# Centring the values before a chunked recurrence, with right sides and outputs split into pieces, in a two-layer RWKV-7 / RetNet trunk

## The chip, the core and the metric

One core of one Trainium2 chip runs the whole program. The time is that of the device, in microseconds (us), the median over runs. The same input is used before and after the change.

## The reference, cut to what matters

Layer 0 mixes tokens by RWKV-7 (16 heads of width 64, 256 tokens, model width 1024), then a dense SwiGLU; layer 1 is a retention mixer and eight experts of which each token uses two. The change is in the RWKV-7 mixer alone:

```python
def step(S, inp):                       # S: 64 x 64 for each head, t = 0 .. 255
    r_t, d_t, k_t, v_t, aa_t, bb_t = inp
    sa = einsum('bhvk,bhk->bhv', S, aa_t)
    S = S * d_t + sa[..., :, None] * bb_t[..., None, :] + v_t[..., :, None] * k_t[..., None, :]
    y = einsum('bhvk,bhk->bhv', S, r_t)
    return S, y
...
mean = jnp.mean(y, axis=-1, keepdims=True)          # group norm over each head's 64 values
var = jnp.mean(jnp.square(y - mean), axis=-1, keepdims=True)
y = (y - mean) * rsqrt(var + 64e-5)
y = y * gn_w + gn_b
bonus = jnp.sum(r * k * r_k, axis=-1, keepdims=True) * v
return ((y + bonus) * g) @ wo
```

The row index v of S is carried through unchanged: S and y are linear in the values v_t, so y minus its mean over the head is what the recurrence gives for values with their mean taken out.

## The kernel before, in words

Everything is float32; matmuls run on TensorE, and the stages follow one another: projections of the RWKV mixer, its recurrence (called the core here), its output projection, the SwiGLU, the retention layer, the experts. The change touches the core, about 95 to 207 us of the span.

**How the core is tiled.** The 256 tokens are four chunks (c = 0 to 3) of 64. Within a chunk the recurrence is a triangular system. Each piece of work on TensorE is a job; the string `order` (before.py, lines 415 to 418) lists the jobs by hand, as name:slot. A slot is a pair of PSUM banks (slot s is banks 2s and 2s + 1). TensorE runs the list in order; a job waits until its inputs are stored and until the job that had its slot before is stored out of PSUM (`slot_free`). VectorE and ScalarE each walk the same list in the same order and do the stores that are theirs (`stores`): VectorE those of M, N, W, Z, Q, S and the last H, ScalarE those of V, B, Y, G and the other H; X and U are split between the two. The names are:

- V0 to V7: value projection, a quarter of 128 tokens each (V0 to V3 the first 128 tokens), stored in `vtok_r`.
- M, N, then W and H: the inverse of the triangular system of chunks 0 and 1 (set 0) and of chunks 2 and 3 (set 1) in six levels; W0.3 is set 0, level 3. The last level is H0.6 and H1.6.
- Q: masked products of keys and queries of a chunk, in two halves. Z: the head sums of the bonus, in 2 tiles. B: four groups of transposed keys.
- X: right side of a chunk, an own part (Q times the chunk's values) and, for c > 0, a part from the state S of the chunk before. U: the solution, written over half of the values' tile `UV`. S: the state after the chunk. Y0, Y1: outputs of chunks 0 and 1, and 2 and 3; each has a part from the states (`state_part`) and a part from Q and `UV`. G0, G1: eight transposes each of the gated, normed output; G0 and G1 feed the output projection `mixer_output`.

**GpSimd** (lines 601 to 661) adds the unit diagonal to the seeds of both inverses (line 619, after N0 and after N1 are stored), scales the keys (line 623), copies the values into `UV` (line 633, four times, a chunk each), and works out the terms of bonus and gate (lines 640 to 644). After Y0 it takes part in the first group norm (lines 648 to 656).

**VectorE** has, beside its stores, two rounds of bonus products (`bonus`, line 1162, after W0.1 and W0.2); after S0 and S1 the decay of the stored state into a spare tile (`St[3]`, line 1265), which the next S store adds to; the first group norm in steps at given jobs (`gn_after`); and the second, from Y1 on, in eight steps (`group_norm`, lines 1169 to 1196). Before G1, TensorE runs `mixer_output(0)` and six eighths of `mixer_output(2)`, 14 products of 128x128 by 128x512.

**SyncE** loads the output weights in two series of eight transfers, each waiting for the one before it (line 550): the first begins when V7 is made, the second not before U1 is made.

## Time and profile before

| | |
|---|---|
| Median of 3 runs | 1593.13 us (1592.57 to 1596.49) |
| The profiled execution: its own time | 1586.79 us |
| Its span | 1584.7 us |
| TensorE busy | 1561.4 us (99%) |
| VectorE busy | 1238.3 us (78%) |
| ScalarE busy | 973.7 us (61%) |
| GpSimd busy | 67.0 us (4%) |
| Granted TensorE clock | 0.998 of full |

PE is TensorE, DVE is VectorE, ACT is ScalarE, POOL is GpSimd, SP is SyncE. In a row of a timeline the first number is the start in us from the span's start, the second the length in us, then engine, line, operation, tiles written and read, shapes, and how many instructions were merged; the bracket gives the idle time just before it and what ended it. Line 1638 is the helper through which all matmuls go, so its rows are told apart by shape and time. A float32 matmul stands as two instructions in the trace. "Issue" is idle time for which the trace shows no other engine as the reason. The profiled execution had a time 6.34 us below the median of the three runs.

### The profile page before, as it was taken

The numbers are of one execution on the slowest core, as the hardware profiler recorded it, in microseconds if no ns is written. First come the engines' busy times: TensorE is split into PE (matmuls) and PEld (weight loads), VectorE is DVE, ScalarE is ACT, GpSimd is POOL, SyncE is SP. The second block draws the span as 40 slices with busy tenths as digits, with TensorE's granted clock in tenths as the row PEclk, the third lists the DMA queues.
The fourth block names the chain that finished last, engine by engine and source line by source line (L and its number), as shares of the span: only waits on it lengthen the run. The fifth ranks groups of instructions, "written<-read, shape, count | busy, mean of one in ns | idle before, by whom it ended". The sixth has DMA issues, their size and how long they took to land.

```text
span 1584.7 us, 24868 instructions
## 1 busy us (share of the span) xinstructions
PE 1561.4 (99%) x9653; PEld 1297.1 (82%) x9653; DVE 1238.3 (78%) x984; ACT 973.7 (61%) x814; POOL 67.0 (4%) x34
## 2 busy tenths in 40 slices
PE   9999899999999999999999999999999999999997
PEld 7778758888998888888888888888888888888885
DVE  7594667774764457989988988988988988988995
ACT  1522345553424446787777777777777777777774
POOL 0043300000000000020000000000000000000200
PEclk9999999999999999999999999999999999999999
DMA  9121259856445525999999999999999999999991
GB/s 317 59 89 30 83 239 366 327 191 231 160 162 197 199 109 184 408 408 385 403 385 362 396 383 364 391 401 353 391 399 351 389 398 354 390 385 360 404 416 63
DMA packets 78588, 470.75 MB, mean 297 GB/s; under 512 B 7860, under 2 KB 8244, under 8 KB 26932
## 3 DMA queue, kind: packets, MB, share of 16 engines
q1 hardware_dynamic: 67860, 442.13, 72.5%
q10 hardware_dynamic: 9504, 23.37, 3.9%
q0 software_dynamic: 1152, 4.19, 0.7%
q8 instruction: 56, 0.92, 0.2%
q14 instruction: 16, 0.13, 0.0%
HBM read 450.27 MB, written 19.40 MB: 296 GB/s over the span
## 4 chain that ended last, share of the span: by engine, by line
PE 93%; DVE 5%; ACT 1%; issue 1%; DMA 0%; POOL 0%; DVEq 0%; SPq 0%; ACTq 0%; POOLq 0%
PE ps L1638 90%; PE ps L2206 2%; DVE mem L1162 1%; PE ps L2198 0%; DMA h<-x 0%; PE ps L1657 0%; DVE mem L1137 0%; ACT mem L760 0%; DVE mem L1145 0%; DVE mem L1134 0%; POOL mem L619 0%; DVE mem L1230 0%; DVE workr L1046 0%; PE ps L1857 0%; ACT work L876 0%
## 5 line engine op out<-in xcount | busy, mean ns | idle before, releaser
L1638 PE MATMUL ps<-pairs_r,workr 128*128 128x512 f32 x2856 | 661.6, 390 | 0.6 <-DVE workr L1380 0.6
L1638 PEld LDWEIGHTS ps<-pairs_r,workr 128*128 128x128 f32 x2856 | 534.8, 188 | 112.2 <-issue 1.1
L1638 PE MATMUL ps<-workr 128*128 128x512 f32 x2024 | 483.4, 393 | 0.0
L1638 PEld LDWEIGHTS ps<-workr 128*128 128x128 f32 x2024 | 375.5, 188 | 77.2 <-DVE workr L1607 0.4
L1544 DVE TENSOR_TENSOR workr<-ring,workr 128x2048 fp32r<-128x2048 f32 x167 | 380.9, 2291 | 52.7 <-ACT workr L958 52.5
L1544 DVE TENSOR_TENSOR pairs_r<-ring,pairs_r 128x2048 fp32r<-128x2048 f32 x165 | 374.0, 2290 | 18.1 <-ACT pairs_r L958 16.2
L958 ACT ACTIVATE pairs_r<-ring 128x2048 fp32r<-128x2048 f32 x165 | 316.9, 1922 | 109.4 <-PE ps L1638 103.9
L958 ACT ACTIVATE workr<-ring 128x2048 fp32r<-128x2048 f32 x167 | 319.3, 1917 | 43.5 <-PE ps L1638 36.2
L1083 DVE TENSOR_TENSOR pairs_r<-ring,pairs_r 128x2048 fp32r<-128x2048 f32 x68 | 155.9, 2292 | 110.3 <-ACT pairs_r L722 108.9
L1638 PE MATMUL ps<-mem 64*64 64x64 f32 (+7 forms) x3064 | 197.7, 260 | 8.0 <-issue 2.6
L722 ACT ACTIVATE pairs_r<-ring 128x2048 fp32r<-128x2048 f32 x65 | 124.5, 1916 | 124.5 <-PE ps L1638 121.5
L1638 PEld LDWEIGHTS ps<-mem 64*64 64x64 f32 (+3 forms) x3064 | 155.2, 147 | 48.7 <-issue 27.2
L1638 PE MATMUL ps<-workr,pairs_r 128*128 128x256 f32 (+1 forms) x1088 | 170.8, 318 | 0.9 <-DVE workr L1046 0.8
L1638 PEld LDWEIGHTS ps<-workr,pairs_r 128*128 128x128 f32 x1088 | 153.4, 189 | 17.9 <-DVE workr L1046 1.4
L963 ACT ACTIVATE workr<-ps 128x512 fp32r<-128x512 f32 x56 | 33.6, 600 | 72.3 <-PE ps L2206 67.3
L1574 DVE TENSOR_TENSOR work<-work,ps 128x512 f32<-128x512 f32 x56 | 38.3, 684 | 25.4 <-PE ps L1638 25.4
L830 ACT ACTIVATE work<-ps 128x512 f32<-128x512 f32 x22 | 13.2, 601 | 53.5 <-PE ps L1638 53.5
L1549 DVE TENSOR_TENSOR workr<-ps,workr 128x512 fp32r<-128x512 f32 x56 | 38.4, 686 | 6.2 <-ACT workr L963 6.2
L736 ACT ACTIVATE mem<-ps 128x512 f32<-128x512 f32 x12 | 6.9, 600 | 43.9 <-PE ps L1638 43.9
L2206 PEld LDWEIGHTS ps<-cst,work 128*128 128x128 f32 x224 | 27.8, 140 | 7.2
L2206 PE MATMUL ps<-cst,work 128*128 128x128 f32 x224 | 33.5, 272 | 0.0
L678 POOL TENSOR_TENSOR route<-route,cst 128x4 f32<-128x4 f32 x1 | 0.2, 198 | 781.6 <-DMA back<-work 781.6
(238 smaller groups left out, 654.8 us busy)
## 6 DMA issues: line engine op xcount, KB each, us to landing
ring<-mstream SPq DMA_DIRECT2D x336, 1024.0 KB, 7.1
ring<-pstream SPq DMA_DIRECT2D x65, 1024.0 KB, 5.0
mem<-rstream SPq DMA_DIRECT2D x27, 512.0 KB, 8.3
sent<-work ACTq DMA_DIRECT2D x6, 1024.0 KB, 8.0
back<-work ACTq DMA_DIRECT2D x6, 1024.0 KB, 11.5
mem<-rstream SPq DMA_DIRECT2D x16, 256.0 KB, 3.4
work<-sent ACTq DMA_DIRECT2D x7, 512.0 KB, 7.8
back<-work ACTq DMA_DIRECT2D x7, 512.0 KB, 9.1
```

Of the source, the lines that this page charges most:

```text
L722: act_f(pair(i)[0], unit(i), ACT.Copy).then_inc(s_hi, 1)
L736: act_f(dst[:, q * 512:(q + 1) * 512], take(j), function).then_inc(s_pe, 1)
L830: act_f(low2[:, f % 2], hidden_banks(f)[:, :, T:2 * T], ACT.Copy).then_inc(s_fc, 1)
L958: act_f(pair(i)[0], unit(i), ACT.Copy).then_inc(s_hi, 1)
L963: act_f(actTh[:, i % 2], ps[:, 6 + i % 2, :].rearrange("p (g s) -> p g s", g=4), ACT.Copy).then_inc(s_ga, 1)
L1083: V.tensor_tensor(pair(i)[1], unit(i), pair(i)[0].bitcast(F32), ALU.subtract).then_inc(s_lo, 1)
L1162: ins = V.scalar_tensor_tensor(out=fm(rT)[:, k, :], in0=fm(rT)[:, k, :], scalar=vec(V_RK, k), in1=fm(kmT)[:, k, :], op0=ALU.mult, op1=ALU. ...
L1544: V.tensor_tensor(pair(i)[1], unit(i), pair(i)[0].bitcast(F32), ALU.subtract).then_inc(s_lo, 1)
L1549: V.tensor_tensor(actTl[:, i % 2], ps[:, 6 + i % 2, :].rearrange("p (g s) -> p g s", g=4), actTh[:, i % 2].bitcast(F32), ALU.subtract).the ...
L1574: V.tensor_tensor(act[:, j % 2, :], s1[:, j % 2, :], ps[:, 2 * (j % 2) + 1, :], ALU.mult).then_inc(s_ma, 1)
L1638: ins = nc.tensor.matmul(*args, **kw)
L2206: ins = nc.tensor.transpose(ps[:, 6 + i % 2, g * P:(g + 1) * P], act[:, i % 2, g * P:(g + 1) * P], ident)
```

## The change

The mean over each head of the values is taken on VectorE (`value_mean`, after the stores of W0.4 and W0.5), and GpSimd subtracts it where it copied values before. The group norms have no mean and no centring any more. ScalarE squares both outputs right behind their stores. VectorE gates the second output beside that. The decay of the state goes to GpSimd (`decayed_state`). The own part of X1 to X3 and the state part of the outputs are items of the order of their own (I1 to I3, P0 and P1), which signal nothing. Order and slots of the jobs are new. Names of semaphores and the tile `vmean` are left out below.

```diff
@@ -410,18 +412,21 @@
-        order = """V0:2 V1:0 M0:1 N0:3 M1:2 V2:0 N1:1 W0.1:3 H0.1:2 V3:0 W0.2:1 Q0.1:3 H0.2:2 V4:0 W0.3:1 H0.3:2
-                   V5:3 W1.1:0 W0.4:1 H1.1:2 Z0:3 V6:0 H0.4:1 W1.2:2 V7:3 W0.5:0 H1.2:1 Z1:2 H0.5:3 Q0.0:0 Q1.0:1
-                   W1.3:2 H0.6:3 B3:0 X0:1 B1:2 H1.3:0 B2:3 B0:1 W1.4:2 U0:0 Q1.1:3 H1.4:1 S0:2 Q2.1:0 X1:3 W1.5:1
-                   U1:2 Q2.0:0 H1.5:3 Y0:1 S1:2 Q3.0:0 H1.6:3 X2:1 Q3.1:2 U2:0 S2:3 X3:2 U3:3 G0:1 Y1:0 G1:1"""
+        order = """V0:2 V1:0 M0:1 N0:3 V2:2 M1:0 W0.1:1 H0.1:3 V3:2 N1:0 W0.2:1 H0.2:3 V4:2 Q0.0:0 W0.3:1 H0.3:3
+                   V5:2 W1.1:0 H1.1:1 W0.4:3 V6:2 H0.4:0 W1.2:1 Q0.1:3 W0.5:2 Z0:0 H0.5:1 H1.2:3 V7:2 W1.3:0 B2:1
+                   H1.3:3 Z1:2 X0:0 H0.6:1 B1:3 W1.4:2 B3:0 Q1.1:1 H1.4:3 U0:2 B0:0 Q1.0:1 W1.5:3 S0:2 Q2.0:0
+                   I1:1 X1:1 P0:3 U1:2 H1.5:0 Q2.1:1 Y0:3 Q3.1:2 I2:0 S1:1 Q3.0:3 H1.6:2 X2:0 I3:1 U2:3 S2:2
+                   X3:1 P1:0 U3:3 G0:1 Y1:0 G1:1"""
         slot_of = {}
...
             slot_of[name[0], int(c), int(n or 0)] = int(s)
-        jobs = list(slot_of)
+        sequence = list(slot_of)
+        jobs = [j for j in sequence if j[0] not in "IP"]
         number = {j: n for n, j in enumerate(jobs)}
-        before = {j: next((i for i in reversed(jobs[:n]) if slot_of[i] == slot_of[j]), None) for n, j in enumerate(jobs)}
+        before = {j: next((i for i in reversed(sequence[:n]) if slot_of[i] == slot_of[j]), None)
+                  for n, j in enumerate(sequence)}
@@ -455,11 +460,8 @@
-        GN_STEPS = 8
-        gn_after = {number["Y", 0, 0]: (0,), number["U", 2, 0]: (1,), number["S", 2, 0]: (2,),
-                    number["X", 3, 0]: (3,)}
-        gn_square_after = number["Y", 0, 0]
-        gn_root_after = number["U", 2, 0]
+        gn_after = {number["Q", 3, 0]: (1,), number["U", 2, 0]: (2,), number["X", 3, 0]: (3,)}
+        gn_root_after = number["X", 2, 0]
@@ -629,9 +631,11 @@
                             pool.wait_ge(*done)
+                    pool.wait_ge(s_vm, c // 2 + 1)
                 r0 = 64 * (c % 2)
-                nc.gpsimd.tensor_copy(UV[r0:r0 + 64, c], vtok_r[r0:r0 + 64, c // 2, :].rearrange(
-                    "p (h v) -> p h v", h=NH)).then_inc(s_uv, 1)
+                nc.gpsimd.tensor_tensor(UV[r0:r0 + 64, c], vtok_r[r0:r0 + 64, c // 2, :].rearrange(
+                    "p (h v) -> p h v", h=NH), vmean[r0:r0 + 64, c // 2].unsqueeze(2).to_broadcast([64, NH, HN]),
+                    ALU.subtract).then_inc(s_uv, 1)
                 pool.wait_ge(s_uv, c + 1)
@@ -644,11 +648,17 @@
-            pool.wait_ge(s_gm0, 1)
-            nc.gpsimd.tensor_tensor(y0, y0, gsum.unsqueeze(2).to_broadcast([P, NH, HN]), ALU.subtract).then_inc(s_gc0, 1)
-            pool.wait_ge(s_gc0, 1)
+            def decayed_state(c):
+                for done in stored(("S", c, 0)):
+                    pool.wait_ge(*done)
+                nc.gpsimd.tensor_tensor(St[3], St[c], gC.rearrange("p (n c) -> p n c", c=NC)[:, :, c + 1:c + 2].to_broadcast(
+                    [P, NP, 64]), ALU.mult).then_inc(s_sg, 1)
+            decayed_state(0)
+            decayed_state(1)
             pool.wait_ge(s_cb, 2)
-            pool.wait_ge(s_gq0, 1)
+            pool.wait_ge(s_gq, 1)
             nc.gpsimd.tensor_tensor(y0f, y0f, gtok[:, 0, :], ALU.mult).then_inc(s_gg0, 1)
@@ -795,11 +805,12 @@
                                   jbank(j, half).rearrange("p (k s) -> p k s", k=4), ACT.Copy).then_inc(s_ygT, 1)
-                if number[j] == gn_square_after:
-                    a.wait_ge(s_gc0, 1)
-                    act_f(UV[:, 0].rearrange("p h v -> p (h v)"), yS[:, 0].rearrange("p h v -> p (h v)"),
-                          ACT.Square).then_inc(s_gq0, 1)
-                    a.preload_act_table(ACT.Sqrt)
+                if kind == "Y":
+                    a.wait_ge(s_ja, count[j, "a"])
+                    act_f(UV[:, 0].rearrange("p h v -> p (h v)"), yS[:, c].rearrange("p h v -> p (h v)"),
+                          ACT.Square).then_inc(s_gq, 1)
+                    if c == 0:
+                        a.preload_act_table(ACT.Sqrt)
                 if number[j] == gn_root_after or j == ("Y", 1, 0):
@@ -1166,56 +1177,50 @@
-            def group_norm(t, step):
-
-                y = yS[:, t]
-                yf = y.rearrange("p h v -> p (h v)")
-                tmp = UV[:, 0]
-                bc = lambda z: z.unsqueeze(2).to_broadcast([P, NH, HN])
-                if step == 0:
-                    for done in stored(("Y", t, 0)):
+            bc = lambda z: z.unsqueeze(2).to_broadcast([P, NH, HN])
+            def value_mean(t):
+                for m in range(4):
+                    for done in stored(("V", 4 * t + m, 0)):
                         v.wait_ge(*done)
-                    link(V.tensor_reduce(gsum, y, AX.X, ALU.add))
-                    link(V.tensor_scalar(gsum, gsum, 1.0 / HN, None, ALU.mult))
-                elif step == 1:
-                    link(V.tensor_tensor(y, y, bc(gsum), ALU.subtract))
-                elif step == 2:
-                    link(V.tensor_tensor(tmp, y, y, ALU.mult))
-                elif step == 3:
-                    link(V.tensor_reduce(gvar, tmp, AX.X, ALU.add))
-                    V.tensor_scalar(gvar, gvar, 1.0 / HN, GN_EPS, ALU.mult, ALU.add).then_inc(s_gv, 1)
...
+                link(V.tensor_reduce(vmean[:, t], vtok_r[:, t, :].rearrange("p (h v) -> p h v", h=NH), AX.X, ALU.add))
+                V.tensor_scalar(vmean[:, t], vmean[:, t], 1.0 / HN, None, ALU.mult).then_inc(s_vm, 1)
+            def group_variance(t):
+                v.wait_ge(s_gq, t + 1)
+                link(V.tensor_reduce(gvar, UV[:, 0], AX.X, ALU.add))
+                V.tensor_scalar(gvar, gvar, 1.0 / HN, GN_EPS, ALU.mult, ALU.add).then_inc(s_gv, 1)
+            def second_group_norm():
+                y, gated = yS[:, 1], UV[:, 1]
+                yf, gf = y.rearrange("p h v -> p (h v)"), gated.rearrange("p h v -> p (h v)")
+                for done in stored(("Y", 1, 0)):
+                    v.wait_ge(*done)
+                v.wait_ge(s_cb, 2)
+                V.tensor_tensor(gf, yf, gtok[:, 1, :], ALU.mult).then_inc(s_gg1, 1)
+                group_variance(1)
+                v.wait_ge(s_gs, 2)
+                rsqrt(gvar, gsd, gsum)
+                v.wait_ge(s_gg1, 1)
+                link(V.tensor_tensor(gated, gated, bc(gsd), ALU.mult))
+                V.tensor_tensor(yf, gf, vtok_r[:, 1, :], ALU.add).then_inc(s_yg[1], 1)
...
                 y = yS[:, 0]
-                if step == 0:
-                    for done in stored(("Y", 0, 0)):
-                        v.wait_ge(*done)
-                    link(V.tensor_reduce(gsum, y, AX.X, ALU.add))
-                    V.tensor_scalar(gsum, gsum, 1.0 / HN, None, ALU.mult).then_inc(s_gm0, 1)
-                elif step == 1:
-                    v.wait_ge(s_gq0, 1)
-                    link(V.tensor_reduce(gvar, UV[:, 0], AX.X, ALU.add))
-                    V.tensor_scalar(gvar, gvar, 1.0 / HN, GN_EPS, ALU.mult, ALU.add).then_inc(s_gv, 1)
+                if step == 1:
+                    group_variance(0)
                 elif step == 2:
                     v.wait_ge(s_gs, 1)
-                    v.wait_ge(s_gc0, 1)
                     rsqrt(gvar, gsd0, gsum, s_gr0)
...
                     yf = y.rearrange("p h v -> p (h v)")
-                    link(V.tensor_tensor(y[:, 8:16], y[:, 8:16], gsd0[:, 8:16].unsqueeze(2).to_broadcast([P, 8, HN]), ALU.mult))
+                    link(V.tensor_tensor(y[:, 8:16], y[:, 8:16], bc(gsd0)[:, 8:16], ALU.mult))
                     v.wait_ge(s_cb, 2)
@@ -1258,20 +1263,18 @@
                     else:
+                        v.wait_ge(s_sg, c)
                         V.tensor_tensor(new, St[3], b3, ALU.add).then_inc(s_jd, 1)
-                    if c < NC - 2:
-                        g = gC.rearrange("p (n c) -> p n c", c=NC)[:, :, c + 1:c + 2].to_broadcast([P, NP, 64])
-                        v.wait_ge(s_jd, count[j, "d"])
-                        link(V.tensor_tensor(St[3], new, g, ALU.mult))
                 elif j == ("G", 1, 0):
...
                                   jbank(j, 1).rearrange("p (k s) -> p k s", k=4)).then_inc(s_ygT, 1)
+                if j in (("W", 0, 4), ("W", 0, 5)):
+                    value_mean(n - 4)
                 if number[j] in gn_after:
...
                 elif j == ("Y", 1, 0):
-                    for step in range(GN_STEPS):
-                        group_norm(1, step)
+                    second_group_norm()
             quarter_add(1, 0)
@@ -1817,6 +1820,19 @@
+            def own_part(job):
+                slot_free(job)
+                c = job[1]
+                wait_stored(("Q", c, 0))
+                wait_stored(("Q", c, 1))
+                pe.wait_ge(s_uv, c + 1)
+                for hd in range(NH):
+                    to, p_ = rows_at(hd % 2, c % 2), hd // 2
+                    ins = M(jbank(job, hd % 2)[to, p_ * 64:(p_ + 1) * 64], Qm[c][:, place(hd), 0:64], UV[:, c, hd, :],
+                            start=(p_ == 0), stop=(c == 0), skip_group_check=True)
+                return ins
             def state_part(job):
@@ -1829,18 +1845,24 @@
-            for j in jobs:
+            for j in sequence:
                 kind, c, n = j
...
                     pe.wait_ge(s_ygT, 2)
-                    wait_stored(("X", 3, 0))
+                    wait_stored(("S", 2, 0))
                     mixer_output(0)
...
                     pe.wait_ge(s_pe, first_in[slot_of[j]])
-                if kind != "Y":
+                if kind == "P":
+                    state_part(j)
+                    continue
+                if kind == "I":
+                    own_part(j)
+                    continue
+                if kind != "Y" and not (kind == "X" and c):
                     slot_free(j)
@@ -1886,14 +1908,9 @@
                 elif kind == "X":
-                    wait_stored(("Q", c, 0))
-                    wait_stored(("Q", c, 1))
-                    pe.wait_ge(s_uv, c + 1)
-                    for hd in range(NH):
-                        to, p_ = rows_at(hd % 2, c % 2), hd // 2
-                        ins = M(jbank(j, hd % 2)[to, p_ * 64:(p_ + 1) * 64], Qm[c][:, place(hd), 0:64], UV[:, c, hd, :],
-                                start=(p_ == 0), stop=(c == 0), skip_group_check=True)
-                    if c:
+                    if c == 0:
+                        ins = own_part(j)
+                    else:
                         wait_stored(("S", c - 1, 0))
@@ -1901,8 +1918,6 @@
                     up = slice(64 * (1 - c % 2), 64 * (1 - c % 2) + 64)
-                    if c == NC - 1:
-                        state_part(("Y", 1, 0))
                     wait_stored(("H", c // 2, LEVELS))
@@ -1912,14 +1927,12 @@
                     if c == 0:
-                        wait_stored(("B", 3, 0))
+                        wait_stored([i for i in jobs if i[0] == "B"][-1])
                     for hd in range(NH):
...
                 elif kind == "Y":
-                    if c == 0:
-                        state_part(j)
                     wait_stored(("U", 2 * c + 1, 0))
```

## Rows read from the trace of the kernel before

**Rows 1.** The chain that ended last: shares of the span by engine.
```profile
PE 93%; DVE 5%; ACT 1%; issue 1%; DMA 0%; POOL 0%; DVEq 0%; SPq 0%; ACTq 0%; POOLq 0%
```

**Rows 2.** Stretches: ends, length, busy us of PE, PEld, DVE, ACT, POOL; PE's clock.
```profile
99.00:192.42 93.42, 85.47 (x2532) 76.62 (x2522) 57.50 (x58) 23.93 (x32) 41.60 (x15) 1.00 0.16 47
...
194.44:206.72 12.28, 12.28 (x34) 5.54 (x31) 9.69 (x13) 1.24 (x2) 0.00 (x0) 1.00 0.01 2
206.72:228.00 21.28, 21.12 (x77) 11.43 (x74) 10.13 (x14) 10.32 (x19) 0.00 (x0) 1.00 0.89 361
```

**Rows 3.** Waits of PE, 99 to 192.42 us: total us, times, longest.
```profile
PE ps L1638 <- issue: 2.6, 4, 1.0
PE ps L1638 <- DVE mem L1250: 1.7, 1, 1.7
PE ps L1638 <- DVE mem L1230: 1.2, 2, 0.6
PE ps L1638 <- DVE mem L1253: 0.9, 1, 0.9
PE ps L1638 <- DVE mem L1241: 0.8, 1, 0.8
```

**Rows 4.** Timeline, start of the core: PE reaches W0.1 (the second row is W0.1).
```profile
97.81 8.29 PE L1638 MATMUL ps<-mem 128*128 128x256 f32 x274
106.50 1.75 PE L1638 MATMUL ps<-mem 64*64 64x64 f32 x105 [0.39 <-POOL mem L619]
```

**Rows 5.** Timeline of POOL.
```profile
102.55 3.81 POOL L619 TENSOR_TENSOR mem<-mem 128x2048 f32<-128x2048 f32 x1 [18.03 <-DVE mem L1236]
...
111.25 5.51 POOL L623 TENSOR_TENSOR mem<-mem,small 128x3072 f32<-128x3072 f32 x1
...
159.47 4.55 POOL L644 TENSOR_TENSOR mem<-mem 128x2048 f32<-128x2048 f32 x1
180.46 2.36 POOL L652 TENSOR_TENSOR mem<-mem 128x1024 f32<-128x1024 f32 x1 [1.26 <-ACT mem L800]
188.00 1.04 POOL L655 TENSOR_TENSOR mem<-mem,small 128x512 f32<-128x512 f32 x1 [5.18 <-DVE small L1036]
```

**Rows 6.** Timeline of DVE: the first bonus products.
```profile
108.86 10.53 DVE L1162 SCALAR_TENSOR_TENSOR mem<-mem,par 128x256 f32<-128x256 f32 x4
```

**Rows 7.** Line 1137 (DVE, beside POOL's 3.64 us memset): min/median/max ns, starts.
```profile
L1137 DVE TENSOR_SCALAR mem<-mem,par x8: 326/344/3682, 80.7 to 85.9; 128x256 f32<-128x256 f32 x8
```

**Rows 8.** Timeline, stores of W1.2, V7, W0.5 and Z1.
```profile
138.80 1.23 DVE L1241 TENSOR_TENSOR mem<-ps,mem 128x1024 f32<-128x1024 f32 x1 [5.44 <-PE ps L1638]
142.43 0.39 ACT L779 ACTIVATE mem<-ps 128x256 f32<-128x256 f32 x1 [3.53 <-PE ps L1638]
143.55 1.23 DVE L1241 TENSOR_TENSOR mem<-ps,mem 128x1024 f32<-128x1024 f32 x1 [3.52 <-PE ps L1638]
...
146.33 0.17 DVE L1228 COPY small<-ps 128x16 f32<-128x16 f32 x1 [1.55 <-PE ps L1638]
```

**Rows 9.** Timeline of DVE and ACT, from after Y0's store to X2's.
```profile
175.79 1.22 DVE L1204 TENSOR_REDUCE small<-mem 128x16 f32<-128x1024 f32 x1 [4.87 <-ACT mem L792]
...
177.84 1.91 DVE L1265 TENSOR_TENSOR mem<-mem,small 128x512 f32<-128x512 f32 x1
179.23 1.06 ACT L800 ACTIVATE mem<-mem 128x1024 f32<-128x1024 f32 x1 [3.48 <-POOL mem L648]
...
182.17 0.69 DVE L1250 COPY mem<-ps 64x512 f32<-64x512 f32 x1
```

**Rows 10.** Timeline, first and last of the second group norm, and G1.
```profile
195.61 1.22 DVE L1178 TENSOR_REDUCE small<-mem 128x16 f32<-128x1024 f32 x1 [3.73 <-ACT mem L792]
...
204.74 1.23 DVE L1196 TENSOR_TENSOR mem<-mem 128x1024 f32<-128x1024 f32 x1
206.56 1.04 PE L1935 MATMUL ps<-cst,mem 128*128 128x128 f32 x8
```

**Rows 11.** Timeline of SP: the 16 transfers of the output weights.
```profile
142.42 48.76 SPq L550 DMA_DIRECT2D mem<-rstream  x16
```

18 lines of the change are left out of this document (5 added, 13 removed).

## The prediction

> **What bounds the kernel now.** I read the chain that ended last first: 93% of the span is TensorE, 5% VectorE [rows 1]. So a change in the core is worth what it does to TensorE's idle time there, and nothing else. I then cut the core into stretches [rows 2]. From 99.00 to 192.42 us, where Y1 begins, TensorE is busy 85.5 of 93.4 us: 8.0 us idle. From 194.44, after Y1, to 206.72 it is busy throughout, with the 14 products placed before G1, and then to 228.00 it idles 0.16 us. All that this change can win from waits lies in those 8.0 us, 0.5% of the time. The waits [rows 3] say whose they are: 2.6 us are "issue", with no engine behind them, and 4.6 us in the four rows of VectorE's stores (lines 1250, 1230, 1253, 1241); the remaining 0.8 us are one wait on GpSimd's seeds of 0.39 [rows 4], one at G0, and rounding. No clock is at stake: it is 1.00 in every stretch [rows 2].
>
> TensorE's work is the same after the change: I and P are parts that stood inside X, U and Y. So time after minus time before is idle after minus idle before, over the same list of jobs. I walk the new order and write down each wait.
>
> **Lengths that the walk uses.** V7 takes 142.43 - 138.80 = 3.6 us, W0.5 1.1 us, H1.2 with Z1 2.8 us [rows 8]; I take 1.1 for each W, H, Q, U, S and part of X, 1.85 for Z, 2.2 for Y and for P1. A full VectorE store is 1.22 to 1.23 us, V's on ScalarE 0.39 [rows 8], half a store of X or U 0.69 [rows 9]. About 0.05 us pass from a job's end to its store, 0.14 from a store to the waiting job (182.17 + 0.69, then the next job at 183.01).
>
> **The start, +1.05 us.** W0.1 begins at 106.50, released by GpSimd's seeds, whose addition starts at 102.55 and lasts 3.81 [rows 4, 5]. That start hangs on N0, which keeps its place. Before, TensorE has M1, V2 and N1 to do in the meantime and waits 0.39. The new order has moved N1 behind V3, so that it waits 0.39 + 1.05 = 1.44 us. The job is not saved, only later.
>
> **Bonus products against GpSimd, -0.4 us.** Four instructions of 0.47 us at the least took 10.53 us [rows 6], while GpSimd ran line 619, line 623 (5.51 us, from 111.25) and two copies back to back [rows 5]; the delay of a store made waits at 119.8 and 122.7 of 0.82 and 0.57 us. With N1 later, the first bonus round (after W0.1, 108.95) meets an idle GpSimd. The second is hit: N1 is made at 106.5 + 2.2 + 0.4 (issue) + 3.6 + 1.1 = 113.8, stored at 115.0, GpSimd then runs 3.81 + 5.51 to 124.4, and the bonus ends at about 125.7. Behind it on VectorE are the stores of Q0.0 (to 126.9) and W0.3 (to 128.1). TensorE meanwhile goes through W0.2, H0.2, V4, Q0.0, W0.3, H0.3, V5 to 126.2 and wants the slot of Q0.0 for W1.1: it waits 0.8, then 0.15 for W0.3's. Sum 0.95, instead of 1.39.
>
> **Value means, +2.2 us.** The first (two instructions, 1.22 [rows 9] and 0.17) follows W0.4's store while TensorE has V6 and H0.4, 4.7 us, before it needs VectorE: nothing. The second is placed after W0.5, but it needs V4 to V7, and V7 comes four jobs later. VectorE stands there; behind it in its queue is the store of Z0, whose slot 0 W1.3 needs, and W1.3 is TensorE's next job after V7. So TensorE stands for 0.05 + 0.39 (V7's store) + 0.05 + 1.22 + 0.02 + 0.17 + 0.17 (Z0's copy) + 0.14 = 2.2 us. Nothing covers it: all that could run in it is behind W1.3. GpSimd's subtraction in place of the copy costs between 1.04 (line 655, half the elements) and 2.36 us (line 652) each [rows 5]; I take 1.9; the first two end near 139, X0 comes near 154, the last two are needed by I2 thirty us later: nothing.
>
> **The tail, +0.1 us.** Before, VectorE carries a reduction and its scaling (1.4 us) and the decay (1.91) between Y0 and the stores that TensorE wants [rows 9], and TensorE waits 1.7, 0.9, 0.7 (issue) and 0.3 there, with 0.6 near 161.5 (line 1230). The new order frees VectorE of those 3.3 us. GpSimd's chain up to line 644 ends near 173 (it took 17.3 us from Z1), then the decay of S0, 1.04 by line 655's row [rows 5], and S1 needs it near 181: hidden. But the variance (1.22 + 0.17) stands after Q3.0 in front of H1.6's store. Count from the start of Q3.1: I2 to 2.1, S1 3.2 (stored 3.95), Q3.0 4.3 (stored 5.6), H1.6 5.4, X2 6.5, I3 7.55. GpSimd decays S1 to 5.15 and gates Y0 until 7.6 (2.36 [rows 5]). VectorE reduces 5.6 to 6.85; its small scaling meets GpSimd. One row shows such an instruction stopped 3.68 us by GpSimd's memset [rows 7], so I let it end at 7.75. Then H1.6's store to 9.0, X2's to 9.65, and U2 starts at 9.8: 2.25 us of wait. S2 follows U2 at once and waits for its store, 0.05 + 0.69 + 0.14 = 0.9, and X3, whose own part I3 is already spent, waits the same 0.9 for S2. Waits of VectorE in the tail: 4.05 us, against 1.7 + 0.9 + 0.6 + 0.3 = 3.5 and 0.4 of other small ones that the new order also covers, together 3.9.
>
> A reduction beside a GpSimd instruction stands in no row; the bounds are 0 (as the stores with one input in PSUM, 1.22 us beside POOL) and 1.25 us more on H1.6's store, were it held until 7.6 like the row of line 1137. I take 0. The Trainium skill, "SBUF — State Buffer", section "Who interferes with whom", says that on trn2 a reduction never contends with GpSimd while a scaling by a constant can; by it the sum stays as I have it, and if it is wrong here the time is that of the second rival below. No row before tests it.
>
> **After Y1, nothing.** The second group norm goes from 195.61 to 205.97 [rows 10]. Reduction, scaling, centring and square, 3.8 us, leave it, a square on ScalarE (1.06 [rows 9]) comes in beside the gating. But the 14 products last until 206.72, later than the norm already, and G1 follows them in TensorE's queue in both kernels. What is late next is TensorE itself: the 3.8 us are worth 0. Were the 14 products not there, they would all count. Output weights: the series takes 48.76 us and its last transfer about 3 [rows 11], from V7's end. V7 is 4.5 us later (146.9), so the end is near 198.5. U1 is also later (173), but the first series lasts until 175. The first use is at Y1's end + 7.0 us, 204: 5 us of cover; without it each us late would count fully.
>
> **Sum.** Issue idle 2.6 is kept: where it falls depends on where code runs out, and I bound it by 0 and 5.2. Changes: +1.05 - 0.45 + 2.2 + 0.15 = +2.95, and about 0.25 for small waits that a tighter list has: +3.2 us. The profiled run took 1586.79 us, so 1590.0 for one like it. The median of the runs shown is 6.34 higher; on it the change gives 1593.13 + 3.2 = **1596.3 us**, 0.2% more.
>
> **Rivals.**
> First, the late stores are swallowed: TensorE does not stand after V7 and before U2, because VectorE, emptied of the means' and decays' work, catches up before TensorE arrives. It would need TensorE to be 2 us slower through H0.5, H1.2 and V7 than 1.1 + 1.1 + 3.6. For it: VectorE is busy 57.5 of 93.4 us only [rows 2]. Against: the order of waits in the queue, which no spare time of VectorE alters. It decides where V7's wait is below 0.2 us. Price 2.2 + 2.25 saved: 3.2 - 4.45 = -1.3, 1591.8 us, faster than before. The floor is all of the waits on stores gone, -4.6 - 0.4: 1588.1.
> Second, reductions contend as well: U2 waits 1.25 more, 1597.6.
> Third, code arrives late more often: the front of the core is denser in small jobs than before, and pauses double: +2.6, 1598.9.
> Fourth, the change does not do what it says to TensorE's order, since other waits than these set the pace: 0, 1593.1.
>
> **Chances.** Forecast 0.50, first rival 0.20, second 0.10, third 0.10, fourth 0.10. A measurement of this kernel can tell about 0.3%, 4.8 us, from no change. Below 1588.3 only the floor gets: 0.04. Above 1597.9: the third rival and the upper edge of the second and of the forecast, 0.16. Within: 0.80. The range, 1590.5 to 1599.5, takes in the first rival's 1591.8 and the third's 1598.9; the forecast's own is 1594.5 to 1597.9.
>
> **What would show it.** TensorE's idle time before Y1's last part 11 us, not 8. A wait of 1.4 us on line 619's successor near 105; VectorE's idle until V7's store and a 2.2 us wait of TensorE behind the copy of Z0; one bonus instruction of over 5 us; two waits of 0.9 at S2 and X3 and one of 2 at U2. G1 straight behind the products, with the norm done 3 us before. If the idle time falls below 8 us the forecast is wrong, whatever else holds; if V7's wait is there and the sum still falls, the tail was misread.

## The result

The changed kernel takes 1593.65 us (median of 20 runs, 1591.24 to 1597.47), beside 1591.82 us of the kernel before in 20 runs on the same chip. The ratio is 1.0017, with an interval of 1.0009 to 1.0025: 2.7 us more by the ratio (the two medians differ by 1.8), slower than before by less than the 0.3% that were called no change. The forecast was +3.2 us, and 1596.3 us in all.

The profiled execution of the changed kernel took 1594.91 us (span 1593.1). That of before took 1586.79, so the two profiles are 8 us apart where the medians are 2 apart. The granted clock of the whole run tells why: 0.992 in this one, 0.998 in that one.

The shares of the chain that ended last, for the changed kernel:

```profile
PE 95%; DVE 2%; ACT 1%; issue 0%; DMA 0%; POOL 0%; DVEq 0%; SPq 0%; ACTq 0%; POOLq 0%
```

And its stretches, with the columns of [rows 2] (ends, length, busy us of PE, PEld, DVE, ACT, POOL, PE's clock, DMA share, GB/s). The first holds the core up to Y1 and a little of the products behind it, the second the products before G1, the third the output projection:

```profile
99.00:199.00 100.00, 90.95 (x2589) 81.65 (x2579) 54.92 (x58) 25.18 (x34) 44.58 (x16) 0.95 0.15 45
199.00:211.10 12.10, 12.10 (x31) 5.36 (x30) 5.75 (x9) 2.29 (x3) 0.00 (x0) 1.00 0.01 2
211.10:232.50 21.40, 21.29 (x77) 11.59 (x75) 10.08 (x14) 10.27 (x19) 0.00 (x0) 1.00 0.88 357
```

TensorE idles 9.05 us in the first, against 8.0 before [rows 2]. The second and third are as before but for 0.2 us. What is new is the eighth number: TensorE had 0.95 of its clock in the core, where it had 1.00. TensorE's waits in that stretch (total us, times, longest) are these:

```profile
PE ps L1641 <- issue: 2.2, 3, 1.1
PE ps L1641 <- DVE small L1233: 2.1, 1, 2.1
PE ps L1641 <- DVE mem L1255: 2.0, 1, 2.0
PE ps L1641 <- DVE mem L1258: 0.9, 1, 0.9
PE ps L1641 <- DVE mem L1267: 0.8, 1, 0.8
PE ps L1641 <- POOL mem L621: 0.6, 1, 0.6
PE ps L1641 <- DVE mem L1235: 0.3, 1, 0.3
```

Beside [rows 3], what is new are two waits of 2 us, one behind V7 and one in front of U2; before, the longest was 1.7. The timeline of the first (start, length, engine, line, operation, and in brackets the idle time before it with its releaser):

```profile
147.59 0.38 ACT L789 ACTIVATE mem<-ps 128x256 f32<-128x256 f32 x1 [2.62 <-PE ps L1641]
148.11 1.22 DVE L1187 TENSOR_REDUCE small<-mem 128x16 f32<-128x1024 f32 x1 [7.40 <-ACT mem L789]
149.36 0.17 DVE L1188 TENSOR_SCALAR small<-small 128x16 f32<-128x16 f32 x1
149.44 0.17 DVE L1233 COPY small<-ps 128x16 f32<-128x16 f32 x1
149.66 1.56 PE L1641 MATMUL ps<-mem 64*64 64x64 f32 x64 [2.11 <-DVE small L1233]
```

This is the walk of the prediction instruction for instruction. VectorE idles 7.40 us until V7 is stored, reduces, scales, copies Z0, and only then TensorE may go on. What follows it is the surprise. The same stretch cut into microseconds, with only length, TensorE's busy time, its clock, DMA share and GB/s as columns:

```profile
148.00:149.00 1.00, 0.00 (x0) 1.00 0.38 88
...
150.00:151.00 1.00, 1.00 (x58) 0.61 0.01 2
151.00:152.00 1.00, 1.00 (x13) 0.50 0.42 131
152.00:153.00 1.00, 1.00 (x16) 0.50 0.36 125
153.00:154.00 1.00, 1.00 (x60) 0.68 0.07 23
154.00:155.00 1.00, 1.00 (x24) 1.00 0.26 68
```

TensorE stands until 149.66, works, and between 150 and 151 is put to 0.50 of its clock, 1.2 instead of 2.4 GHz, until after 153. The granted clock falls after the wait, not in it. Summed as one minus the clock over the four lines, the fall comes to 1.7 us on top of the wait's 2.1. On the same work it cost 1.5: from the end of this wait to the transposes of B1 TensorE took 8.54 us (149.66 to 158.20), and 7.04 (148.94 to 155.98) in a kernel below in which no fall follows. The same comes again in the tail:

```profile
186.83 1.22 PE L1641 MATMUL ps<-mem 64*64 64x64 f32 x32 [2.02 <-DVE mem L1255]
188.93 1.98 PE L1641 MATMUL ps<-mem 128*64 128x64 f32 x32 [0.88 <-DVE mem L1258]
191.69 4.32 PE L1641 MATMUL ps<-mem 64*64 64x64 f32 x128 [0.78 <-DVE mem L1267]
```

U2, S2 and X3 wait 2.02, 0.88 and 0.78 us. S2's 32 instructions take 1.98 us; at full clock they took 1.15 in the run with both moves below. The clock is 0.50 from 188 to 194, which over TensorE's busy time sums to 2.6 us. The work itself, the three rows above, took 7.52 us instead of 5.73 in the run with both moves: 1.8 us more.

### The profile page after: what moved, and what is told of

It reads as the page before. It is cut to its first block, busy times and chain, and to the rows that moved or that the text cites. A ratio compares the mean times of both kernels' runs of the same rounds, so it can differ in the third digit from the quotient of the medians.

```text
span 1593.1 us, 24870 instructions
## 1 busy us (share of the span) xinstructions
PE 1570.0 (99%) x9653; PEld 1305.8 (82%) x9653; DVE 1231.9 (77%) x980; ACT 974.0 (61%) x815; POOL 68.6 (4%) x35
## 4 chain that ended last, share of the span: by engine, by line
PE 95%; DVE 2%; ACT 1%; issue 0%; DMA 0%; POOL 0%; DVEq 0%; SPq 0%; ACTq 0%; POOLq 0%
PE ps L1641 92%; PE ps L2219 2%; DVE mem L1173 1%; PE ps L2211 0%; DMA h<-x 0%; PE ps L1660 0%; PE ps L1879 0%; POOL mem L621 0%; PE ps L2148 0%; DVE workr L1057 0%; ACT work L887 0%; DVE work L1375 0%; DVE mem L1241 0%; DVE mem L1235 0%; DVE h L1615 0%
## 5 line engine op out<-in xcount | busy, mean ns | idle before, releaser
L1641 PE MATMUL ps<-mem 64*64 64x64 f32 (+6 forms) x3064 | 200.7, 265 | 9.5 <-issue 2.2
```

Source lines behind the costliest of these rows:

```text
L1641: ins = nc.tensor.matmul(*args, **kw)
```

## The experiments

**Theory A:** the change adds two long waits of TensorE, and each costs its own length and a stretch at half clock behind it; the places alone decide. **Rival B:** the granted clock falls now and then in any run, wherever it likes, and the profile after happened to catch two falls. Both explain the 8 us between the profiles; they differ in what a kernel without the long waits would do. A single profile's fall can be chance, so the clocks of all runs are set side by side at the end. The first four kernels take away one wait, the other, both, and put a shorter one back.

**The mean of the second half later.** It stands behind W1.3, which runs after V7's store in any case; no work is left out.

```diff
-                if j in (("W", 0, 4), ("W", 0, 5)):
-                    value_mean(n - 4)
+                if j in (("W", 0, 4), ("W", 1, 3)):
+                    value_mean(c)
```

> Of the changed kernel, one placement is moved: VectorE takes the mean of the second half of the values after its store of W1.3 instead of after W0.5, so it no longer stands for V7 with Z0's copy behind it. Theory A (a wait of about 2 us also halves the granted clock for some 3 us behind it; in the changed kernel's trace the clock is 0.50 to 0.68 from 150 to 154 us, right behind the 2.11 us wait): the wait of 2.1 us goes and the granted clock stays 1.00 in the four us after V7, worth 2.1 + 1.7 = 3.8 us against the changed kernel; the second dip, at 187 to 195 us, stays. Ratio to the kernel before about 1.0017 - 0.0024 = 0.9993. Rival B (the clock dips come of themselves, wherever they fall): only 2.1 us go, a dip shows somewhere in the core all the same, ratio about 1.0004.

Measured: 1591.36 us, ratio 0.9997 [0.9986, 1.0008], which is 3.2 us under the changed kernel's ratio. The interval holds A's 0.9993 and B's 1.0004; the profile speaks for A. The wait behind V7 is gone and the clock stays at 1.00 there; the wait before U2 is 2.0 us as before, and the fall behind it is there (stretches of this kernel, columns as above):

```profile
144.00:154.00 10.00, 10.00 (x227) 8.85 (x223) 2.71 (x5) 3.26 (x5) 2.04 (x2) 1.00 0.18 56
184.00:195.00 11.00, 9.34 (x196) 8.88 (x197) 4.48 (x10) 1.54 (x3) 2.31 (x2) 0.53 0.31 96
```

**The variance later.** The other wait alone.

```diff
-        gn_after = {number["Q", 3, 0]: (1,), number["U", 2, 0]: (2,), number["X", 3, 0]: (3,)}
-        gn_root_after = number["X", 2, 0]
+        gn_after = {number["X", 2, 0]: (1,), number["S", 2, 0]: (2,), number["X", 3, 0]: (3,)}
+        gn_root_after = number["U", 2, 0]
```

> Of the changed kernel, one placement is moved: the variance of the first output is taken on VectorE after the store of X2 instead of after Q3.0, its root on ScalarE after U2, its reciprocal root after S2. The stores of H1.6 and X2 are then not held up. Theory A: U2's wait falls from 2.02 to about 0.2 us, the clock stays 1.00 from 187 to 195 us, worth 1.8 + 2.4 (dip of 0.5 to 0.88 over eight us, less the part of it in which TensorE waited) = 4.2 us at most, part of which comes back if G0 now waits for the norm, by up to 1.5 us; the dip behind V7 stays. Ratio to the kernel before about 1.0000. Rival B: 1.8 us less of wait and a dip all the same, ratio about 1.0006.

Measured: 1592.91 us, 1.0006 [0.9992, 1.0019], which is B's number, with A's 1.0000 inside the interval. The profile is the mirror image: U2's wait is 0.2, the tail runs at 1.00, and the fall behind V7 stays. The gain is smaller, as 0.9 us of it come back as a wait of G0, which needs the norm that was moved back; and the profile has one more fall, at 157.5 to 160.7, with no long wait ahead of it.

```profile
150.00:154.00 4.00, 4.00 (x104) 3.47 (x94) 1.23 (x1) 0.90 (x2) 3.11 (x2) 0.57 0.22 70
182.00:194.00 12.00, 9.60 (x336) 8.78 (x332) 9.54 (x15) 2.39 (x6) 6.04 (x4) 1.00 0.28 90
```

**Both later.** Both edits above.

> Both placements moved (the second mean after W1.3, the variance after X2). Theory A: no dip of the clock in the core at all, as in the profile of the kernel before; against the changed kernel 2.1 + 1.8 us of wait and about 1.7 + 2.4 us of clock less, some 7 to 8 us; ratio to the kernel before about 1.0017 - 0.0048 = 0.9970, 2.7 to 4.5 us faster than it. Rival B: the waits alone, ratio about 0.9993.

Measured: 1589.12 us, 0.9978 [0.9965, 0.9991]: 6.2 us less than the changed kernel, and faster than before. A's 0.9970 is inside the interval and B's 0.9993 just outside. Neither place has a fall. But A had forecast none in the core, and there is one at 141 to 145, in which TensorE never stood still:

```profile
182.00:196.00 14.00, 11.09 (x281) 9.22 (x277) 8.24 (x14) 5.02 (x8) 2.97 (x3) 1.00 0.28 93
141.00:145.00 4.00, 4.00 (x131) 3.83 (x127) 0.10 (x1) 1.62 (x2) 0.00 (x0) 0.57 0.01 4
```

**VectorE held for V7, with nothing to do there.** The kernel with both moves, and VectorE waits for V7's store after W0.5 as in the changed one, but does no reduction.

```diff
+                if j == ("W", 0, 5):
+                    for done in stored(("V", 7, 0)):
+                        v.wait_ge(*done)
```

> As the kernel with both placements moved, but VectorE still waits for the store of V7 after W0.5, with nothing to do there but the copy of Z0 behind it: TensorE waits 0.05 + 0.39 + 0.05 + 0.17 + 0.14 = 0.8 us instead of 2.1 behind V7. It is the same place with a shorter wait. Theory A, that the length of the pause decides: 0.8 us slower than the kernel with both moved and no dip of the clock. Rival C, that any pause at this place brings the dip (with the same work before it): 0.8 + 1.7 = 2.5 us slower, and a clock of about 0.57 over the four us behind V7.

Measured: 1590.67 us, 0.9988 [0.9977, 1.0000]. The wait is back at 0.68 us, without the reduction's 1.4, and no fall follows it. So the order of waits makes the hold and the reduction makes it long; that only the long one touches the clock rests here on one profile. In time the step from the kernel with both moves is 1.6 us with overlapping intervals, so that it decides between neither A's 0.8 nor C's 2.5.

```profile
148.94 1.16 PE L1644 MATMUL ps<-mem 64*64 64x64 f32 x64 [0.68 <-DVE small L1233]
```

**The kernel before, with the hold built in.** If A is right, a wait of 2 us put into the kernel before must bring the fall as well.

```diff
+                if j == ("W", 1, 2):
+                    for done in stored(("V", 7, 0)):
+                        v.wait_ge(*done)
+                    link(V.tensor_reduce(small[:, 224:240], ...))
+                    V.tensor_scalar(small[:, 224:240], small[:, 224:240], 1.0 / HN, None, ALU.mult).then_inc(s_hold, 1)
...
+                if j == ("W", 0, 5):
+                    pe.wait_ge(s_hold, 1)
```

> The kernel before with a pause put in and nothing else: behind V7, VectorE waits for its store, reduces the second half of the values into spare columns and scales them, as the changed kernel does, and TensorE waits for that before W0.5. The wait is 0.05 + 0.39 + 0.05 + 1.22 + 0.02 + 0.17 + 0.14 = 2.0 us. Theory A (a wait of about 2 us brings a dip of the granted clock right behind it, worth 1.7 us, on top of its own length): 3.7 us slower than before, ratio 1.0023, and clock 0.5 to 0.7 in the three to four us after the wait. Rival B (dips fall where they like, waits do not bring them): 2.0 us slower, ratio 1.0013, mean granted clock of the runs as before (0.9944).

Measured: 1597.42 us, 1.0039 [1.0023, 1.0056], +6.2 us. B's 1.0013 is outside the interval, and A's 1.0023 is its lower end. The wait came out at 2.80 us, not 2.0, and the timeline shows who took the 0.8:

```profile
143.00 2.14 POOL L634 COPY mem<-mem 64x1024 f32<-64x1024 f32 x2 [23.93 <-ACT mem L780]
144.13 1.04 DVE L1274 TENSOR_SCALAR small<-small 128x16 f32<-128x16 f32 x1
145.22 4.97 PE L1644 MATMUL ps<-mem 64*64 64x64 f32 x140 [2.80 <-DVE small L1274]
```

The scaling, 0.17 us by itself, ends when GpSimd's copies do. The clock then falls twice, from 145 to 149 and from 151 to 156, and a third time, from 189 to 193, behind the tail's wait, which was 1.71 us before and is 1.95 here. Two more waits are new or longer, of 1.3 us (on ScalarE, at 168) and 1.1 us (before G0, 0.3 in the kernel before), so that the 6.2 us are not those of one wait and its fall. This kernel's stretch:

```profile
144.00:156.00 12.00, 10.78 (x292) 10.41 (x296) 4.43 (x6) 2.05 (x2) 6.01 (x4) 0.72 0.30 92
```

**A new tail.** The kernel with the later mean, and H1.6 moved ahead of I2 and Q3.1 behind X2, so that the variance stands after H1.6's store and none that TensorE wants is behind it.

```diff
-                   I1:1 X1:1 P0:3 U1:2 H1.5:0 Q2.1:1 Y0:3 Q3.1:2 I2:0 S1:1 Q3.0:3 H1.6:2 X2:0 I3:1 U2:3 S2:2
+                   I1:1 X1:1 P0:3 U1:2 H1.5:0 Q2.1:1 Y0:3 H1.6:2 I2:0 S1:1 Q3.0:3 X2:0 Q3.1:2 U2:3 S2:2 I3:1
...
-        gn_after = {number["Q", 3, 0]: (1,), number["U", 2, 0]: (2,), number["X", 3, 0]: (3,)}
-        gn_root_after = number["X", 2, 0]
+        gn_after = {number["H", 1, 6]: (1,), number["U", 2, 0]: (2,), number["X", 3, 0]: (3,)}
+        gn_root_after = number["H", 1, 6]
```

> The changed kernel with the second mean after W1.3, and the end of the order rewritten so that each store in the chain S1, X2, U2, S2, X3 has a job beside it: Y0, H1.6, I2, S1, Q3.0, X2, Q3.1, U2, S2, I3, X3. The variance follows the store of H1.6, which now comes before S1. Expected waits of TensorE: U2 about 0.2, S2 about 1.05 (the store of Q3.1 stands in front of U2's), X3 and G0 none, so about 1.7 us less wait than in the kernel with both placements moved. Theory: ratio to the kernel before about 0.9978 - 0.0011 = 0.9967. Rival: if dips of the clock set the medians and not waits below 1 us, no difference to the kernel with both moved, 0.9978.

Measured: 1586.49 us, 0.9967 [0.9953, 0.9982], 5.3 us faster than before. That is the ratio forecast, but the kernel with both moves (0.9978) lies inside the interval. The waits of U2 and X3 are gone; what is left, beside the pauses, is one wait of a microsecond and three shorter ones, of which the longest is shown:

```profile
PE ps L1641 <- issue: 4.3, 5, 1.4
PE ps L1641 <- DVE mem L1258: 1.0, 1, 1.0
PE ps L1641 <- POOL mem L621: 0.6, 1, 0.6
```

**The pieces in the order of before.** Centred values, right sides and outputs in pieces and the decay by GpSimd stay; order and banks are those of before, with each I ahead of its X, the variance after U2, its root after S2.

> All parts of the change (values centred, squares on ScalarE, state decayed by GpSimd, means on VectorE after W0.4 and W0.5) in the job order and slots of before; own and state parts stand directly at their jobs, as they did. The variance is taken after U2's store and the reciprocal root after S2's, as before. In this order V7 comes before W0.5, so the second mean has nothing to wait for. Theory: VectorE's 3.3 us between Y0 and H1.6's store are gone, so the wait for X2's store (1.7) goes; the others stay (0.39, 0.82, 0.57, 0.58, 0.9, issue 2.6): idle 6.1 instead of 8.0 us, ratio 0.9988. It would say that the parts alone gain and the new order loses. Rival: the new order is what lets the parts pay (own parts ahead of the wait on the state): then idle stays near 8 us and the ratio at 1.000 or above.

Measured: 1587.59 us, 0.9972 [0.9957, 0.9987], better than expected. So the pieces help by about 4.5 us. Where all of it comes from is not shown: from 99 us to G1 TensorE idles 6.9 us in this profile against 8.0, where 6.1 was forecast. The changed kernel gives that gain up and 2.7 us more. It isn't the new order as such that takes them: with only the two placements moved, the new order stands at 0.9978, with intervals that overlap.

**The same with the decay on VectorE again.**

```diff
-            decayed_state(0)
-            decayed_state(1)
...
+                    if c < NC - 2:
+                        ...
+                        link(V.tensor_tensor(St[3], new, g, ALU.mult))
```

> As the kernel with all parts in the old order, but the two decays of the state are back on VectorE behind the stores of S0 and S1. Theory: once the reduction and centring are gone, VectorE has room for the decay (0.69 us each when GpSimd is idle, 1.9 at most when its product by the gate stands in front) before H1.6's and X2's stores; no wait comes back and the ratio stays at 0.9972 within 0.0005. Rival: moving the decay to GpSimd is what removed the wait for X2's store; then 1.7 us come back with a dip behind them, ratio 0.9985 to 0.9995.

Measured: 1589.88 us, 0.9982 [0.9968, 0.9997]. The intervals overlap, so that the time alone doesn't tell it apart from the one before; the timeline does:

```profile
163.22 4.54 POOL L648 TENSOR_TENSOR mem<-mem 128x2048 f32<-128x2048 f32 x1
...
164.46 3.85 DVE L1268 TENSOR_TENSOR mem<-mem,small 128x512 f32<-128x512 f32 x1
...
170.30 0.92 PE L1642 MATMUL ps<-mem 64*64 64x64 f32 x24 [2.42 <-DVE mem L1253]
```

The decay of S0 starts inside GpSimd's instruction and takes 3.85 us. In the kernel before it took 0.69, at 164.02, as GpSimd's chain ended in that moment; here the chain runs until 167.76, in part because two subtractions take 3.9 us where two copies took 2.1. The stores behind the decay are late, TensorE waits 2.42 for X1's, and from 171.5 to 175 its clock is at half:

```profile
171.00:175.00 4.00, 4.00 (x96) 3.71 (x93) 2.19 (x3) 0.59 (x1) 0.00 (x0) 0.57 0.24 70
```

X2's store, where the rival had put the wait, is free: the decay of S1 took 0.69. With centred values this order wants the decay on GpSimd; that is read from one profile of each kernel and not from the time.

**A longer second norm.** The new tail's kernel, with three products of 1.22 us more in the second group norm.

```diff
+                spare = UV[:, 2]
+                for _ in range(3):
+                    link(V.tensor_tensor(spare, y, y, ALU.mult))
```

> The kernel with the new tail, and three products of 128x1024 (1.22 us each, written to a spare tile) put into VectorE's second group norm, 3.7 us in all, as much as the change took out there. Theory (the 14 products before G1 hide the norm): its end moves from about 201.6 to 205.3 us, still before the products end at about 206.6; G1 starts where it did, ratio as without it, 0.9967. Rival (the shorter second norm is worth its length): 3.7 us slower, 0.9990.

Measured: 1586.76 us, 0.9973 [0.9961, 0.9986], against 0.9967 without: 1.0 us by the ratios, inside the error, and less than the rival's 3.7 (one run of 6304.5 us is left out). The norm ends at 204.39, still ahead of the products, and G1 follows them:

```profile
195.26 3.74 DVE L1206 TENSOR_TENSOR mem<-mem 128x1024 f32<-128x1024 f32 x3
...
203.16 1.23 DVE L1212 TENSOR_TENSOR mem<-mem 128x1024 f32<-128x1024 f32 x1
...
205.07 1.04 PE L1951 MATMUL ps<-cst,mem 128*128 128x128 f32 x8
```

**N1 early again.** The new tail's kernel with N1 straight behind M1, as before.

```diff
-        order = """V0:2 V1:0 M0:1 N0:3 V2:2 M1:0 W0.1:1 H0.1:3 V3:2 N1:0 W0.2:1 H0.2:3 V4:2 Q0.0:0 W0.3:1 H0.3:3
+        order = """V0:2 V1:0 M0:1 N0:3 V2:2 M1:0 N1:1 W0.1:0 H0.1:3 V3:2 W0.2:1 H0.2:3 V4:2 Q0.0:0 W0.3:1 H0.3:3
```

> The kernel with the new tail, with N1 back ahead of W0.1 (slots: N1 in 1, W0.1 in 0). TensorE then has N1 to do while GpSimd adds the first seeds, so that the wait of 0.6 to 1.3 us ahead of W0.1 falls to about 0.3; the second seeds and the key scaling now stand in front of the first bonus round, but TensorE has V3, H0.2, V4 and Q0.0 beside it. Theory: 0.5 to 1.2 us less, ratio 0.9960 to 0.9964. Rival: the saved wait comes back at W0.3 or the inverse's next level, as in the kernel before (0.82 us for line 1241), ratio 0.9967.

Measured: 1585.65 us (8 runs), 0.9965 [0.9949, 0.9980], not told apart from 0.9967, nor the theory from its rival. The wait before W0.1 is 0.41 us (the last row), and its span, 1581.3 us, is the lowest of all profiles here.

```profile
PE ps L1641 <- issue: 2.5, 4, 1.3
...
PE ps L1641 <- DVE mem L1241: 0.4, 1, 0.4
```

**Both kernels once more.** Each was profiled a second time, unchanged, to see what repeats.

> The kernel before, unchanged, for a second profile of it: its first profile shows a granted clock of 1.00 throughout and took 1586.8 us, while its median lies near 1592. Theory A: in a run of the usual length the granted clock dips somewhere, for 5 to 9 us at half in total length of loss, most of it at 610 to 632 us (routing, where the changed kernel's profile has 0.56 and 0.93), and the core shows none or one short dip behind the wait of 1.7 us near 183 us.

> The changed kernel, unchanged, for a second profile. Theory: both waits of about 2 us are there again, behind V7 and before U2, and the granted clock is at half for three us or more behind each. Rival: the dips move, and one of the two waits has a clock of 1.00 behind it.

The kernel before took 1590.68 us (span 1588.7). Its 1.7 us wait in the tail, after which the first profile kept 1.00, is now followed by a fall (first row), and there is another from 620 to 627, as forecast. The changed kernel took 1592.98 us; both its long waits and both falls are there again (second and third row).

```profile
183.00:190.00 7.00, 6.12 (x110) 5.84 (x112) 4.50 (x9) 0.81 (x2) 0.63 (x1) 0.51 0.34 107
```

```profile
151.00:155.00 4.00, 4.00 (x98) 3.48 (x89) 1.23 (x1) 1.04 (x2) 3.03 (x2) 0.57 0.27 83
188.00:196.00 8.00, 6.34 (x160) 6.04 (x157) 3.94 (x9) 1.18 (x2) 2.31 (x2) 0.57 0.32 102
```

**What the profiles say together.** Waits of TensorE of 1.95 us or more stand in six of the fourteen, nine in all (two each in both profiles of the changed kernel and in the kernel before with the hold, one each in the later mean, the later variance and the decay on VectorE). After all nine the clock was at half for 3 us or more; the falls begin between the last 0.2 us of the wait and 1.6 us behind it. The 1.7 us wait of before: one of two. The 0.68 us wait: none. This is A. But falls without a long wait stand in many profiles too: at 141 to 146 us in five (both later, new tail, longer second norm, N1 early, and the second profile of the changed kernel), at 131 to 139 (pieces in the old order), 147 to 152 (decay on VectorE), 151 to 156 (the hold) and 157 to 161 us (later variance) in one each, and near 620 us, behind the core, in ten. For those B holds, and what brings them is open.

**The clock over all runs.** Each run lists its mean granted clock. The mean over runs of time × (1 − clock) is the time lost to it, and time × clock what it would be at full clock (an estimate, as not all work scales with TensorE):

| Kernel | runs | mean us | lost | at full clock |
|---|---|---|---|---|
| before (three later groups) | 88 | 1591.7 | 8.7 | 1583.0 |
| changed | 20 | 1594.0 | 11.6 | 1582.5 |
| later mean | 12 | 1591.1 | 10.1 | 1581.0 |
| later variance | 12 | 1592.1 | 9.7 | 1582.4 |
| both later | 12 | 1588.6 | 7.2 | 1581.5 |
| both later, short hold | 12 | 1589.7 | 8.0 | 1581.8 |
| before, with the hold | 11 | 1597.0 | 11.9 | 1585.1 |
| new tail | 12 | 1586.5 | 6.2 | 1580.3 |
| the same, longer norm | 11 | 1587.0 | 6.5 | 1580.5 |
| the same, N1 early | 8 | 1585.4 | 5.7 | 1579.7 |
| pieces, old order | 12 | 1587.2 | 6.9 | 1580.3 |
| the same, decay on VectorE | 12 | 1589.6 | 7.2 | 1582.4 |

The standard error of a loss is 0.3 us for before, 0.5 for the changed kernel and the later mean, 0.6 to 0.9 for the others and 1.4 for the hold. The loss goes with the long waits: 11.6 us with both, about 10 with one, 7.2 with none and 8.0 with the short hold; and from 8.7 to 11.9 where the hold is put into the kernel before. This rests on all runs and not on one profile each, and it is the best evidence for A here.

The loss overstates what the clock costs, for two reasons. In every profile 3 to 4 us of it lie behind TensorE's last product, where a low clock costs nothing; that is much the same in all kernels. And work takes less than twice as long at half clock. Before's own runs show it: the 13 with a clock of 0.997 or more lost 4.0 us and took 1588.4 in the mean, the 12 with 0.992 or less lost 13.3 and took 1594.9, which is 0.7 us of time for a us of loss. Its two profiles agree, here from 99 us to G1 (the first row is the first profile):

```profile
99.00:206.56 107.56, 99.61 (x2625) 83.95 (x2616) 67.19 (x71) 26.26 (x36) 41.60 (x15) 1.00 0.14 42
99.00:208.32 109.32, 101.36 (x2627) 86.07 (x2618) 66.53 (x71) 26.21 (x36) 41.24 (x15) 0.97 0.14 42
```

TensorE idles 8.0 us in both, and the second is 1.8 us longer for a loss of 3.0 us in busy time.

The changed kernel loses 2.8 us more to the clock than before, so about 2 us of time by that rate (an estimate). Its idle time up to G1 is 9.1 and 8.7 us in its two profiles, against 8.0 and 7.9: about 0.9 us more. Together that is 2.9, beside 2.7 measured: some two thirds are the clock's and one third is idle time.

## Why the prediction was right, and where it wasn't

The difference was right: +3.2 forecast, +2.7 [1.4, 4.0] measured, in the case that had most of the chance. The total of 1596.3 us was 2.7 too high, in part since it stood on a median of three runs of before, 1593.13, where twenty gave 1591.82; 1593.65 is inside the range and a little below the 1594.5 at which the forecast's own part of it began. The single waits of the core's second half were right too. That the sum agreed was luck: two errors met. The idle time was put 2.1 us too high, and the clock, worth about 2 us, was put at nothing.

- **Value means.** Forecast 2.2 us behind V7; 2.11 measured, by the steps that were written down. Its place and cause are shown by the later mean and by the hold without the reduction.
- **The tail.** 2.25, 0.9 and 0.9 forecast; 2.02, 0.88 and 0.78 measured. The scaling did meet GpSimd and the reduction did not, as the timeline of the changed kernel shows:

```profile
182.44 2.36 POOL L662 TENSOR_TENSOR mem<-mem 128x1024 f32<-128x1024 f32 x1
182.89 1.21 DVE L1193 TENSOR_REDUCE small<-mem 128x16 f32<-128x1024 f32 x1
184.13 0.70 DVE L1194 TENSOR_SCALAR small<-small 128x16 f32<-128x16 f32 x1
```

 The reduction took 1.21 us in the middle of GpSimd's instruction, as without it; the scaling ended with it. What the Trainium skill says, as the prediction weighed it ("SBUF — State Buffer", "Who interferes with whom"), agrees with both, and the second rival, with reductions held, is refuted.
- **Bonus products.** The end was forecast at 125.7 and came at 125.62. One round was free, the other stretched over GpSimd's chain:

```profile
109.41 1.66 DVE L1173 SCALAR_TENSOR_TENSOR mem<-mem,par 128x256 f32<-128x256 f32 x4
...
116.23 9.39 DVE L1173 SCALAR_TENSOR_TENSOR mem<-mem,par 128x256 f32<-128x256 f32 x4
```

 The longest instruction of the second took 5.55 us ("one of over 5 us" was the sign to look for). TensorE came to W1.1 0.3 us later than walked and the store of Q0.0 was 0.15 earlier, so the waits were 0.27 us and not 0.95.
- **The start.** Forecast 1.44 us; 0.63 in the first profile, since a pause of 1.10 us had just delayed TensorE, and 1.3 in the second. The mechanism is right and the size is at its upper end. A pause can stand in for part of a wait, as here, which a sum that adds both doesn't see.
- **After Y1 nothing.** In the changed kernel the norm ends at 206.4 and G1 starts at 211.10. The 3.7 us put back into the norm cost 1.0 us by the ratios, inside the error. The output weights never held TensorE.
- **Idle time.** 11.2 us forecast, 9.05 measured: the start is 0.8 too long, the bonus 0.7, the tail 0.4, pauses 0.4, small waits 0.25. (These come to 2.5 and not to 2.1, as the waits that the prediction names for the kernel before come to 8.3 and not to 8.0.) TensorE's busy time less the loss came out 0.8 us shorter than before (86.65 against 87.48 us from 99 us to Y1's end), where the work was taken as the same. That is no gain of the change: the second profile of the kernel before, on the same work, falls short of the first by 1.2 us, as its clock fell. The loss takes off more than the clock cost.
- **The step that failed** is "No clock is at stake: it is 1.00 in every stretch". That was the state of one execution, at 0.998 one of the fastest that before has. In the changed kernel's profile the two falls in the core come to 1.7 + 2.6 = 4.3 us as one minus the clock, and to 1.5 + 1.8 = 3.3 us on the same work. With the 3.3 us and the walk as it stood, the forecast would have said +6.5 us and been too high; with the walk corrected by its 2.1 us, it is +4.4 beside the full-clock run of before, and G1 does start 4.5 us later (211.10 against 206.56). The rest of the 8 us between the two profiles lies mostly outside the change: near 620 us the changed kernel's profile has another fall, 0.56 from 620 to 630. The usual run of before has falls of its own, so that the medians differ by less.

Of the rivals, the first (late stores swallowed) is refuted, as both stores held TensorE for 2 us. The third (twice the pauses) isn't seen: 2.2 us against 2.6, and between 1.2 and 4.3 over all kernels, 1.2 in the second profile of this very one. That pauses come from code arriving late is shown by no run. The fourth would have given the same median within 2.7 us, yet its reason is wrong: the waits forecast are there.

## What to carry to other kernels

A reduction on an engine's queue costs what stands behind it, from the moment its last operand lands: place it after the job that makes that operand, and after the stores that TensorE needs next. Price a wait of TensorE of 2 us at nearly twice its length here (2.1 + 1.5 us behind V7, 2.0 + 1.8 in the tail), and short waits, of which the one tested had 0.7 us, at their lengths; several short ones beat one long one. Before the words "no clock is at stake", look at the clock of every run and not at one profile's. And take the price of a fall from the same work at both clocks: the sum of one minus the clock was too high by 0.2 of 1.7 and by 0.8 of 2.6 us.

## What the runs showed of the hardware

- TensorE's granted clock went to 0.50 after nine of nine waits of 1.95 us or longer, for 3 us or more each time, and also in stretches in which TensorE was busy all the time (4.00 of 4.00 us at a mean clock of 0.57). The Trainium skill, "TensorE: Matmul & The Clock Gate", "What's actually happening", says that "the default state is throttled, and activity releases the throttle". The falls behind waits agree; those in busy stretches are not what that sentence alone would give.
- Of VectorE's operations on tiles outside PSUM, a reduction was not held by GpSimd's (1.21 us), the others shown here were: a scaling of 0.17 us took 0.70 and 1.04, a decay of 0.69 took 3.85, and a round of four bonus products, 1.66 us when GpSimd was idle, took 9.39. Copies on GpSimd held the scaling (1.04 us) as its product did (0.70).
- A fall cost less time than half clock would take off: 1.5 us for a loss of 1.7, 1.8 for 2.6 and 1.8 for 3.0, each on the same work.
- Pauses of TensorE with nothing behind them, up to 1.4 us each, sum to between 1.2 and 4.3 us in the core, and differ by 1.0 us between two profiles of one kernel (2.2 and 1.2).
